# Inverting triangular matrices on a matrix engine: from 128x128 products to pairs of 64x64 blocks

## The reference, cut to what matters

```python
def step(S, inp):
    r_t, k_t, v_t, w_t, kk_t, a_t = inp
    sa = jnp.einsum('bhvk,bhk->bhv', S, -kk_t)
    S = (S * w_t[:, :, None, :]
         + sa[..., None] * (kk_t * a_t)[:, :, None, :]
         + v_t[..., None] * k_t[:, :, None, :])
    y = jnp.einsum('bhvk,bhk->bhv', S, r_t)
    return S, y
...
_, y = lax.scan(step, S0, xs)
```

## Time and profile before

| | |
|---|---|
| median of 3 runs | 944.76 us (944.45 to 944.95) |
| span of the profiled execution | 943.0 us |
| PE busy | 909.9 us (96%) |
| PEld busy | 799.4 us (85%) |
| DVE busy | 685.4 us (73%) |
| ACT busy | 513.4 us (54%) |
| POOL busy | 96.6 us (10%) |

### The profile page before, as it was taken

The page is one execution under the profiler, slowest core; times in us unless marked ns, Lnnn a source line. Parts: engine busy times, 40 slices in busy tenths (PEclk is TensorE's granted clock), DMA queues, the critical chain, the costliest instruction groups (busy, mean ns, idle before and its releaser), DMA issues.

```text
span 943.0 us, 14451 instructions
## 1 busy us (share of the span) xinstructions
PE 909.9 (96%) x5705; PEld 799.4 (85%) x5705; DVE 685.4 (73%) x970; ACT 513.4 (54%) x734; POOL 96.6 (10%) x91
## 2 busy tenths in 40 slices
PE   6999999999999989999999899999999998999998
PEld 6998998988888769999988689988878786878777
DVE  6688836783878678888863667787687687776665
ACT  6863332233555366656643655766475667477543
POOL 6002421430000000000000000006320000000000
PEclk9999999999999999999999999999999999999999
DMA  9543132212465364665655544643223453632231
GB/s 307 169 148 107 59 107 62 84 46 90 159 220 178 135 220 138 201 201 179 200 201 180 178 135 140 201 160 131 90 91 129 151 178 131 205 123 90 90 110 69
DMA packets 80979, 136.63 MB, mean 145 GB/s; under 512 B 3957, under 2 KB 46545, under 8 KB 80912
## 3 DMA queue, kind: packets, MB, share of 16 engines
q1 hardware_dynamic: 78800, 131.17, 42.1%
q0 software_dynamic: 2112, 4.53, 1.5%
HBM read 134.64 MB, written 1.05 MB: 144 GB/s over the span
## 4 chain that ended last, share of the span: by engine, by line
PE 63%; DVE 6%; ACT 5%; issue 3%; DMA 1%; DVEq 0%; ACTq 0%
PE bank L437 18%; PE bank L439 17%; PE bank L438 17%; PE bank L426 3%; DVE lower L1861 2%; ACT upper L1297 2%; PE bank L1076 1%; PE bank L881 1%; PE bank L889 1%; PE bank L1060 1%; DVE arena L2401 1%; ACT arena L1777 1%; PE bank L684 1%; DMA loaded<-in_ffn_w_up 1%; DMA loaded<-in_ple_gate_w 1%
## 5 line engine op out<-in xcount | busy, mean ns | idle before, releaser
L1861 DVE TENSOR_TENSOR lower<-loaded,upper 128x2048 fp32r<-128x2048 f32 x122 | 279.7, 2296 | 123.6 <-ACT upper L1297 121.5
L1297 ACT ACTIVATE upper<-loaded 128x2048 fp32r<-128x2048 f32 x122 | 231.9, 1903 | 115.3 <-PE bank L439 101.5
L437 PE MATMUL bank<-xT_upper,upper 128*128 128x256 f32 (+1 forms) x664 | 187.4, 282 | 2.0 <-DVE xT_lower L1926 1.8
L438 PE MATMUL bank<-xT_lower,upper 128*128 128x256 f32 (+1 forms) x664 | 185.7, 280 | 0.0
L439 PE MATMUL bank<-xT_upper,lower 128*128 128x256 f32 (+1 forms) x664 | 185.6, 280 | 0.0
L437 PE MATMUL bank<-upper,xT_upper 128*128 128x512 f32 (+1 forms) x360 | 146.2, 406 | 4.7 <-DVE lower L1861 3.5
L439 PE MATMUL bank<-upper,xT_lower 128*128 128x512 f32 (+1 forms) x360 | 139.8, 388 | 0.0
L438 PE MATMUL bank<-lower,xT_upper 128*128 128x512 f32 (+1 forms) x360 | 139.3, 387 | 0.0
L437 PEld LDWEIGHTS bank<-xT_upper,upper 128*128 128x128 f32 (+1 forms) x664 | 125.8, 190 | 3.3 <-issue 2.7
L438 PEld LDWEIGHTS bank<-xT_lower,upper 128*128 128x128 f32 (+1 forms) x664 | 125.9, 190 | 0.1
L439 PEld LDWEIGHTS bank<-xT_upper,lower 128*128 128x128 f32 (+1 forms) x664 | 125.9, 190 | 0.1
(11 more groups left out here) (340 smaller groups left out, 1209.4 us busy)
## 6 DMA issues: line engine op xcount, KB each, us to landing
loaded<-in_w_in SPq DMA_DIRECT2D x26, 1024.0 KB, 5.1
loaded<-in_ffn_w_up SPq DMA_DIRECT2D x22, 1024.0 KB, 5.1
loaded<-in_ssm_in_w SPq DMA_DIRECT2D x20, 1024.0 KB, 5.3
loaded<-in_ffn_w_down SPq DMA_DIRECT2D x11, 1024.0 KB, 5.0
loaded<-in_ssm_out_w SPq DMA_DIRECT2D x8, 1024.0 KB, 5.0
loaded<-in_ple_gate_w SPq DMA_DIRECT2D x8, 1024.0 KB, 5.1
loaded<-in_attn_in_w SPq DMA_DIRECT2D x8, 1024.0 KB, 5.2
loaded<-in_w_branch_ret SPq DMA_DIRECT2D x4, 1024.0 KB, 5.0
```

The costliest lines, as they stand in the source:

```text
L437: mm(out, a[0], b[0], start=start, stop=False)
L438: mm(out, a[0], b[1], start=False, stop=False)
L1297: A(part(upper, PARTS, n), part(loaded, LOADS, n), ACT.Copy).then_inc(uppers, 1)
L1861: TT(part(lower, LOADS, n), part(loaded, LOADS, n), part(upper, PARTS, n).bitcast(F32), sub) \
```

## The change

Levels 1 to 5 work on the two 64x64 diagonal blocks alone. `inv`, `invT`, `t1` and `lk` become 64 columns wide: rows 0 to 63 hold the first block, rows 64 to 127 the second. A new helper `blocks` issues, for each head, one product for rows 0 to 63 (output on partitions 0 to 63) and one for rows 64 to 127 (output on partitions 64 to 127), so on opposite quarters of the array, both into the same PSUM bank. There is one bank for each of `t1`, `x` and `xt` in place of two. Level 6 is one 64x64 block: `t1` from rows 0 to 63 to partitions 64 to 127, and `xt` the other way. The full transposed inverse is put together in `invTw`; its lower left corner is cleared once by POOL. `L` is made as 64x64 blocks as well. ACT has one copy for each level instead of two, DVE two additions instead of four (three at level 5, one copy at level 6), and POOL masks half the rows at a time, two instructions for each level, for levels 1 to 5, into one of two buffers. The quarters of `dense` stay where they were. The table of constants is 512 columns narrower.

```diff
-    for k in range(LEVELS):
-        same = (row >> (k + 1)) == (col >> (k + 1))
-        parts[f"off{k}"] = same & (((col >> k) & 1) == 1) & (((row >> k) & 1) == 0)
-    parts["off0L"] = parts["off0"].T
+    row6, col6 = row % 64, col[:, :64]
+    for k in range(LEVELS - 1):
+        same = (row6 >> (k + 1)) == (col6 >> (k + 1))
+        parts[f"off{k}"] = same & (((col6 >> k) & 1) == 1) & (((row6 >> k) & 1) == 0)
+    parts["off0L"] = (row6 >> 1 == col6 >> 1) & (col6 & 1 == 0) & (row6 & 1 == 1)
+    parts["ident6"] = (row6 == col6)
...
-        inv, invT, t1, lk = ar(23056, 8, P), ar(24080, 8, P), ar(25104, 8, P), ar(11280, 8, P)
+        inv, invT, invTw, t1 = ar(23056, 8, 64), ar(23568, 8, 64), ar(24080, 8, P), ar(25104, 8, 64)
+        both_inv, lk = ar(23056, 16, 64), ar(11280, 2, 8, 64)
...
+            def blocks(key, bank, a, b):
+                ps = take(pe, key, bank)
+                for hd in range(8):
+                    for r in (slice(0, 64), slice(64, P)):
+                        last = mm(ps[r, 64 * hd:64 * hd + 64], a[r, hd, :], b[r, hd, :], start=True, stop=True)
+                fill(last, key)
...
@@ -657,33 +669,37 @@
                         r = slice(64 * o, 64 * o + 64)
                         ps = take(pe, ("L", n, o), 4 + o)
                         for p in range(4):
-                            last = mm(ps[:, P * p:P * p + P], zr[r, p, n, 0:P], bt[r, p, n, :], start=True, stop=True)
+                            for b in range(2):
+                                c = slice(64 * b, 64 * b + 64)
+                                last = mm(ps[c, 64 * p:64 * p + 64], zr[r, p, n, c], bt[r, p, n, c], start=True, stop=True)
                         fill(last, ("L", n, o))
                 dense(("L", n))
                 pe.wait_ge(sem("inv_start"), n + 1)
-                for k in range(1, LEVELS):
-                    for q in range(2):
-                        pe.wait_ge(sem("lk_ready"), 12 * n + 2 * (k - 1) + q + 1)
-                        if k > 1:
-                            emptied(pe, ("x", n, k - 1, q), ("xt", n, k - 1, q))
-                        ps = take(pe, ("t1", n, k, q), 4 + q)
-                        for e in range(4):
-                            last = mm(ps[:, P * e:P * e + P], lk[:, 4 * q + e, :], inv[:, 4 * q + e, :],
-                                      start=True, stop=True)
-                        fill(last, ("t1", n, k, q))
+                for k in range(1, LEVELS - 1):
+                    pe.wait_ge(sem("lk_ready"), 10 * n + 2 * k)
+                    if k > 1:
+                        emptied(pe, ("x", n, k - 1))
+                    blocks(("t1", n, k), 4, lk[:, k % 2, :, :], inv)
                     dense(("t", n, k))
-                    for q in range(2):
-                        emptied(pe, ("t1", n, k, q))
-                        for key, a, b, bank in ((("x", n, k, q), invT, t1, 2 * q), (("xt", n, k, q), t1, invT, 2 * q + 1)):
-                            if key[0] == "x" and k == LEVELS - 1:
-                                continue
-                            ps = take(pe, key, bank)
-                            for e in range(4):
-                                hd = 4 * q + e
-                                last = mm(ps[:, P * e:P * e + P], a[:, hd, :], b[:, hd, :], start=True, stop=True)
-                            fill(last, key)
+                    emptied(pe, ("t1", n, k))
+                    if k > 1:
+                        emptied(pe, ("xt", n, k - 1))
+                    blocks(("x", n, k), 0, invT, t1)
+                    blocks(("xt", n, k), 1, t1, invT)
                     dense(("x", n, k))
+                emptied(pe, ("x", n, 5))
+                ps = take(pe, ("t1", n, 6), 4)
+                for hd in range(8):
+                    last = mm(ps[64:P, 64 * hd:64 * hd + 64], mats[0:64, hd, 0, 64:P], inv[0:64, hd, :], start=True, stop=True)
+                fill(last, ("t1", n, 6))
+                dense(("t", n, 6))
+                emptied(pe, ("t1", n, 6), ("xt", n, 5))
+                ps = take(pe, ("xt", n, 6), 1)
+                for hd in range(8):
+                    last = mm(ps[0:64, 64 * hd:64 * hd + 64], t1[64:P, hd, :], invTw[64:P, hd, 64:P], start=True, stop=True)
+                fill(last, ("xt", n, 6))
+                dense(("x", n, 6))
                 if n:
                     pe.wait_ge(sem("qk_rope"), 2)
-                emptied(pe, ("rhs", n), ("xt", n, LEVELS - 1, 0), ("xt", n, LEVELS - 1, 1))
+                emptied(pe, ("rhs", n), ("xt", n, 6))
+                if n == 0:
+                    pe.wait_ge(sem("corner_clear"), 1)
...
-                    last = mm(ps[:, 64 * hd:64 * hd + 64], invT[:, hd, :], rhs[:, 64 * hd:64 * hd + 64],
+                    last = mm(ps[:, 64 * hd:64 * hd + 64], invTw[:, hd, :], rhs[:, 64 * hd:64 * hd + 64],
...
+            pool.memset(invTw[64:P, :, 0:64], 0.0).then_inc(sem("corner_clear"), 1)
+            def level_masked(n, k, r):
+                pool.tensor_tensor(lk[r, k % 2, :, :], mats[r, :, 0, r], const(f"off{k}")[r].unsqueeze(1).broadcast_to([64, 8, 64]),
+                                   ALU.mult).then_inc(sem("lk_ready"), 1)
             for n in range(2):
-                for k in range(1, LEVELS):
+                for k in range(1, LEVELS - 1):
                     if k == 1:
                         pool.wait_ge(sem("mats_ready"), 8 * (n + 1))
-                    for q in range(2):
-                        if k > 1:
-                            full(pool, ("t1", n, k - 1, q))
-                        elif n:
-                            full(pool, ("t1", 0, LEVELS - 1, q))
-                        pool.tensor_tensor(lk[:, 4 * q:4 * q + 4, :], mats[:, 4 * q:4 * q + 4, 0, :],
-                                           const(f"off{k}").unsqueeze(1).broadcast_to([P, 4, P]), ALU.mult) \
-                            .then_inc(sem("lk_ready"), 1)
+                        if n:
+                            full(pool, ("t1", 0, 4))
+                            full(pool, ("t1", 0, 5))
+                    if k > 2:
+                        full(pool, ("t1", n, k - 2))
+                    level_masked(n, k, slice(0, 64))
+                    level_masked(n, k, slice(64, P))
...
-                    for q in range(2):
-                        copy(t1[:, 4 * q:4 * q + 4, :], ("t1", n, k, q))
+                    ps = full(act, ("t1", n, k))
+                    r = slice(0 if k < 6 else 64, P)
+                    empty(A(t1[r, :, :], ps[r, :].rearrange("p (a b) -> p a b", a=8), ACT.Copy), ("t1", n, k))
...
-                    empty(TT(iv[:, :, o, :], four(ps), bc(const("off0L").unsqueeze(1), P, 4, P), mul), ("L", n, o))
-                TT(invT[:, :, :], mats[:, :, 0, :], bc(const("off0").unsqueeze(1), P, 8, P), mul).then_inc(sem("inv_masked"), 1)
+                    empty(TT(iv[:, :, o, :], ps[:, 0:256].rearrange("p (a b) -> p a b", a=4),
+                             bc(const("off0L").unsqueeze(1), P, 4, 64), mul), ("L", n, o))
+                for r in (slice(0, 64), slice(64, P)):
+                    TT(invT[r, :, :], mats[r, :, 0, r], bc(const("off0")[r].unsqueeze(1), 64, 8, 64), mul) \
+                        .then_inc(sem("inv_masked"), 1)
                 emptied(ve, ("L", n, 0), ("L", n, 1))
-                ve.wait_ge(sem("inv_masked"), n + 1)
-                TT(inv[:, :, :], inv[:, :, :], bc(ident.unsqueeze(1), P, 8, P), add).then_inc(sem("inv_halves"), 1)
-                ve.wait_ge(sem("inv_halves"), n + 1)
-                TT(invT[:, :, :], invT[:, :, :], bc(ident.unsqueeze(1), P, 8, P), add).then_inc(sem("inv_start"), 1)
+                ve.wait_ge(sem("inv_masked"), 2 * n + 2)
+                TT(both_inv, both_inv, bc(const("ident6").unsqueeze(1), P, 16, 64), add).then_inc(sem("inv_start"), 1)
                 dense(("L", n))
                 ve.wait_ge(sem("inv_start"), n + 1)
                 for k in range(1, LEVELS):
-                    for q in range(2):
-                        for key, dst in ((("x", n, k, q), inv), (("xt", n, k, q), invT)):
-                            if key[0] == "x" and k == LEVELS - 1:
-                                continue
-                            ps = full(ve, ("xt", n, k, q))
-                            ps = full(ve, key)
-                            d = dst[:, 4 * q:4 * q + 4, :]
-                            empty(TT(d, d, four(ps), add), key)
-                        if k < LEVELS - 1:
-                            emptied(ve, ("x", n, k, q))
-                        emptied(ve, ("xt", n, k, q))
+                    eight = lambda ps: ps.rearrange("p (a b) -> p a b", a=8)
+                    if k < 6:
+                        ps = full(ve, ("x", n, k))
+                        empty(TT(inv[:, :, :], inv[:, :, :], eight(ps[:, :]), add), ("x", n, k))
+                    ps = full(ve, ("xt", n, k))
+                    if k < 5:
```

(11 more changed lines are left out.)

## The result

| | before | after |
|---|---|---|
| median | 944.61 us (943.67 to 944.95, 4 runs) | 922.96 us (921.99 to 923.96, 4 runs) |
| span of the profiled execution | 943.0 us | 920.1 us |
| PE busy, records | 909.9 us | 887.1 us, 6217 |
| DVE busy | 685.4 us | 671.3 us |

The ratio is 0.9771, with an interval of 0.9757 to 0.9784. The forecast was 925.0 us, faster, in a range of 914 to 938. The span fell by 22.9 us. The median lies 2.9 us above it (1.8 before), since the profiled execution was the quickest of the four.

What follows compares the result with a forecast made beforehand. PE was taken as the bound, at 96% over the span. Terms of -25.8, -3.4, +9.4, -0.3 and +0.3 gave -19.8 us, so 923.2 from 943.0 and a median of 925.0 us, range 914 to 938.

Steps and rivals of the forecast that it cites:

- Pairs: Levels 1 to 5: two 64x64 records on opposite quarters overlap fully, 480 pairs at 0.058 us, a gain of 25.8 us.
- Trips: PE going from 128-row tiles to 64-row tiles and back, 24 times at 0.39 us: 9.4 us lost.
- Levels 1 to 5: Products of both chunks: 53.6 us fall to 27.8, less 20 moves into the half-row tile and back at 0.39 us.
- PE's waits for DVE: Second chunk: PE's wait of about 1.3 us for DVE neither goes nor grows; bounds 0 and 4 us.
- Level 6: 64 records, now 64x64 on one quarter without overlap: 7.1 us fall to 3.7, a gain of 3.4 before tile changes.
- The start of a chunk: DVE's shorter chain to `inv_start` saves PE 0.3 us in both chunks together, no more.
- L: Made as 64x64 blocks, counted at nothing; bounds a gain of 0.9 us and a loss of 1.2.
- No overlap: Rival: the two records of a pair run one after the other, +6.5 us, 951 us; chance 0.13 together with dear loads.
- Partial overlap: Rival: a record in levels 1 to 5 costs 0.035 to 0.045 us, giving 930 to 940 us; chance 0.15.
- dear loads: Rival: loads of 64 columns cost as much as of 128, giving 953 us; chance 0.13 together with no overlap.
- DVE as the bound: Rival: DVE bounds the second chunk, 2 to 4 us more, 927 to 929; counted within full overlap's 0.62.
- Cheaper trips: Rival: tile changes cost up to 9.4 us less on PE, DVE takes 2 to 3 back, 918 us; chance 0.07.

Runs made afterwards that it cites:

- halves_in_turn: The changed kernel with each block issuing all 16 records for rows 0 to 63 first, then the 16 for rows 64 to 127: 943.54 us, ratio 0.9987.
- Experiment 6: The changed kernel with POOL masking a level only after t1 of the level before, not one level earlier: 924.45 us, ratio 0.9788.
- experiment 4: The changed kernel with both dense quarters of levels 1 to 5 behind t1 and none behind xt: 927.68 us, ratio 0.981.
- probe_32: The changed kernel with an extra block of 64 records of 32x32 at levels 1 to 4, its result unread: 929.63 us in one run.
- two small-block kernels: The changed kernel with levels 1 to 4 on four 32x32 blocks: 925.15 us; the same with seven dense quarters moved into the levels: 923.51 us.

## Why the prediction was right, point by point

- **Pairs** (480 x 0.058, full overlap): right, 0.058 measured, by the mean of a block. The ground was right as well: `halves_in_turn` shows what happens without it.
- **Trips** (24 x 0.39): 0.36 in the timeline, 0.34 in the run that adds ten. The term was 0.7 us too large.
- **Levels 1 to 5** together: 18.0 us less were expected (25.8 - 20 x 0.39). Measured 9.43 in the first chunk and 10.70 in the second, 20.1.
- **PE's waits for DVE** are the step that failed, and the largest part of that difference. The prediction said they "neither go nor grow"; they went. The second chunk's levels had 1.3 us more than the first's, and now have the same 31.3. I walked through DVE's list with the durations of before. But the rotation got faster: its lines took 15.9 us in all instead of 18.7. Experiment 6 shows that this comes of when POOL makes its masks: made late, they bring back 1.4 us of waiting ahead of the same `t1`. A duration read beside a busy neighbour isn't a property of the instruction, and this change moved the neighbour. The wait in the first chunk (+0.3) didn't come either.
- **Level 6** (-3.4 + 4 x 0.39 = -1.8): measured -1.13 and -1.12, 2.25 together.
- **The start of a chunk** (-0.3): 0. The two maskings (1422 ns in the mean, for 512 elements on half the partitions) took longer than the one of 1024 that they replace, 1.2 us, and the identity addition kept its 2.1 us, though the same addition takes 1.23 with no mask beside it (experiment 6). The prediction had POOL's early masks as hidden and did not ask what they cost DVE. PE waits 0.35 for the addition; it was 0.17 before.
- **`L`** at nothing: its blocks take half of the 0.9 us, but with its own change of tile no gain came out that I can tell from the rows between the chunks (28.76 us before, 28.82 after).
- **Behind the recurrent part** 0.5 us were gained that no step had.
- The sum: 9.43 + 10.70 + 2.25 + 0.5 is 22.9, where 19.8 were forecast. The 925.0 for the median came closer than the span's 923.2 against 920.1, since the median lay 2.9 us above the span and not 1.8: part of the miss was made good by chance.
- **The rivals.** *No overlap* was the right one to fear: with the records in another order it came true, at 943.5 us. *Partial overlap* and *dear loads* fell with the 0.058 of a pair. *DVE as the bound* came true only in part, when DVE's cover was taken away (experiment 4) or POOL's masks came late (experiment 6). *Cheaper trips* fell.

## What to carry to other kernels

Products that filled half of the array or less cost nothing here as partners, but only if the instruction stream brings them in turns; a run of more than a few on one half puts them in a row again. Before cutting blocks further, divide PE's instructions by the time they will take: where a few hundred come within a few us, what was saved in the array can be lost waiting for instructions. And when a change moves the work of one engine, take its neighbours' durations as bounds, not as constants.

## What the hardware showed that was not expected

- Column halves over the same 64 rows overlap too: 16 records of `L` at 0.029 us each.
- Four diagonal quarters of 32x32 run at once: 64 records in 0.53 us (`probe_32`).
- PE started a record of the other half only when three of this half were left (`halves_in_turn`, 88.044 us).
- PE can be short of instructions: pauses of 0.4 to 2.9 us inside blocks of records, 10.0 us in all, at 408 instructions in a level of 5.1 us; none at 216 in 6.3, nor at 344 in the 6.9 of `probe_32`. All twelve pauses of the two small-block kernels stand whole blocks of some 254 instructions apart and end 1.2 to 1.6 us after a 16 KB packet of instructions has landed. Behind the longest ones the granted clock was 0.50 for some 2 us.
- DVE's durations depend on when POOL works: one instruction of line 2127 takes 0.69 us with no mask beside it and 1.65 to 1.79 with one; an addition that reads PSUM took 0.69 either way.
